# Layer 1's first norm in two halves, and three filter products moved into its gaps

## The reference

```
hl = modulate(rmsnorm(xl, norm1_g[l]), mod_l[0], mod_l[1])      # latent
hc = modulate(rmsnorm(xc, norm1_g[l]), mod_c[0], mod_c[1])      # context
hy_l, pool_l, cq_l, ckv_l, kpe_l = split(hl @ w_in[l])
hy_c, pool_c, cq_c, ckv_c, kpe_c = split(hc @ w_in[l])
k, v from ckv, kpe of both; attention, Hyena convolution and pooling, then w_out, gated residual add
rmsnorm, modulate, channel mixing: dense SwiGLU in layer 0, top-2 of 8 experts in layer 1
```

## Time and profile before

| | |
|---|---|
| median of 3 runs | 1709.87 us (1708.15 to 1710.27) |
| profiled execution | 1708.7 us, span 1706.8 us |
| TensorE matmul busy | 1618.1 us, 95% of the span |
| VectorE busy | 1294.3 us, 76% |
| ScalarE busy | 891.7 us, 52% |
| mean granted clock of TensorE | 0.977 of full speed |

### The profile page before, as it was taken

The page is one execution under the profiler, slowest core; times in us unless marked ns, Lnnn a source line. Parts: engine busy times, 40 slices in busy tenths (PEclk is TensorE's granted clock), DMA queues, the critical chain, the costliest instruction groups (busy, mean ns, idle before and its releaser), DMA issues.

```text
span 1706.8 us, 19495 instructions
## 1 busy us (share of the span) xinstructions
PE 1618.1 (95%) x7452; PEld 1273.2 (75%) x7452; DVE 1294.3 (76%) x1733; ACT 891.7 (52%) x1019; POOL 14.1 (1%) x30
## 2 busy tenths in 40 slices
PE   5998999899999999798789999999999999999996
PEld 2885668678788887685487778787887878788774
DVE  3844573797787756854668998898988889898897
ACT  3322372322222222434557777777777776777764
POOL 1000000000000000000000000000000000000000
PEclk9999999899999999899889999999999999999999
DMA  9226421444445553132137999999999999999992
GB/s 391 81 78 236 147 80 50 172 182 169 173 172 200 220 199 122 34 114 94 61 149 285 352 343 337 346 356 359 351 334 362 347 355 346 343 347 370 344 347 107
DMA packets 55971, 403.43 MB, mean 236 GB/s; under 512 B 6416, under 2 KB 6448, under 8 KB 8768
## 3 DMA queue, kind: packets, MB, share of 16 engines
q1 hardware_dynamic: 53712, 387.47, 60.5%
q0 software_dynamic: 2160, 14.63, 2.3%
HBM read 401.03 MB, written 1.05 MB: 236 GB/s over the span
## 4 chain that ended last, share of the span: by engine, by line
PE 76%; DVE 15%; ACT 5%; issue 3%; DMA 1%; SPq 0%; DVEq 0%; ACTq 0%
PE PS L439 20%; PE PS L441 20%; PE PS L440 20%; DVE w_lo L2254 6%; ACT w_hi L1480 3%; PE PS L737 2%; DVE arena L1616 1%; DVE w_lo L1603 1%; PE PS L993 1%; PE PS L762 1%; PE PS L749 1%; DMA arena<-in_ada 1%; PE PS L698 1%; PE PS L449 1%; PE PS L704 1%
## 5 line engine op out<-in xcount | busy, mean ns | idle before, releaser
L2254 DVE TENSOR_TENSOR w_lo<-arena,w_hi 128x2048 fp32r<-128x2048 f32 x132 | 301.7, 2290 | 43.9 <-ACT w_hi L1480 43.9
L2254 DVE TENSOR_TENSOR w_lo<-raw,w_hi 128x2048 fp32r<-128x2048 f32 x129 | 295.0, 2291 | 32.8 <-ACT w_hi L1480 32.4
L1480 ACT CAST w_hi<-arena 128x2048 fp32r<-128x2048 f32 x132 | 251.6, 1909 | 47.0 <-PE PS L441 47.0
L1480 ACT CAST w_hi<-raw 128x2048 fp32r<-128x2048 f32 x129 | 246.9, 1916 | 44.4 <-PE PS L441 44.4
L439 PE MATMUL PS<-hT_hi,w_hi 128*128 128x512 f32 (+1 forms) x576 | 217.6, 378 | 12.2 <-DVE hT_lo L1751 10.6
L440 PE MATMUL PS<-hT_lo,w_hi 128*128 128x512 f32 (+1 forms) x576 | 214.6, 373 | 0.0
L441 PE MATMUL PS<-hT_hi,w_lo 128*128 128x512 f32 (+1 forms) x576 | 214.4, 372 | 0.0
L439 PE MATMUL PS<-w_hi,hT_hi 128*128 128x512 f32 (+1 forms) x448 | 178.3, 398 | 0.3 <-DVE w_lo L2254 0.3
L441 PE MATMUL PS<-w_hi,hT_lo 128*128 128x512 f32 (+1 forms) x448 | 174.6, 390 | 0.0
L440 PE MATMUL PS<-w_lo,hT_hi 128*128 128x512 f32 (+1 forms) x448 | 173.5, 387 | 0.0
L1603 DVE TENSOR_TENSOR w_lo<-raw,w_hi 128x2048 fp32r<-128x2048 f32 (+1 forms) x54 | 122.3, 2266 | 34.8 <-ACT w_hi L1109 34.6
(11 more groups left out here) (320 smaller groups left out, 2520.2 us busy)
## 6 DMA issues: line engine op xcount, KB each, us to landing
raw<-in_moe SPq DMA_DIRECT2D x132, 1024.0 KB, 6.9
arena<-in_moe SPq DMA_DIRECT2D x132, 1024.0 KB, 6.9
raw<-in_ffn SPq DMA_DIRECT2D x33, 1024.0 KB, 4.8
raw<-in_dot SPq DMA_DIRECT2D x28, 1024.0 KB, 4.8
raw<-in_ada SPq DMA_DIRECT2D x17, 1024.0 KB, 7.3
raw<-in_out SPq DMA_DIRECT2D x8, 1024.0 KB, 4.8
raw<-in_inb SPq DMA_DIRECT2D x8, 960.0 KB, 4.8
raw<-in_ina SPq DMA_DIRECT2D x5, 1024.0 KB, 5.4
```

The costliest lines, as they stand in the source:

```text
L1480: nc.scalar.copy(w_hi[:, x_slot(j), :], x_raw(n)).then_inc(x_hi, 1)
L2254: v.tensor_tensor(w_lo[:, x_slot(j), :], x_raw(NGR * (i % 2) + j), w_hi[:, x_slot(j), :].bitcast(F32), ALU.subtract).then_inc(x_lo, 1)
```

## The change

- Layer 1's first norm treats the latent stream of all eight blocks, and the projection to u waits for these alone. The context's half is a second pass of the same code on ScalarE and VectorE, behind the convolutions and behind the split of the third B granule; ScalarE's shift copies come behind it.
- The B products with b = 1 take the latent tiles first, then the context's. Their PSUM banks are named outright; the spread's bank is now 7, since the context's pass still reads it. A context tile waits for the low halves of the four blocks that it reads.
- Steps 8 to 10 of layer 1's filter leave the feed-forward network: TensorE does step 8 ahead of the norm's column sums, step 9 between sums and spread, step 10 behind the spread. ScalarE's copies of step 8 stand behind the square root, those of 9 and 10 behind the latent half of the norm.
- Two calls that split weights within the norm go away, and events carry the stream's number.

```diff
-    return n if b % 3 == 0 and 3 <= n <= 10 else None
+    return n if b % 3 == 0 and 3 <= n <= 7 else None
...
+        def own_tiles(l, b):
+            return (0, 1, 2, 3) if l == 0 else (2, 3, 0, 1) if b else (2, 3)
...
-                b = 7 if l else None
+                b = {8: 0, 9: 3, 10: 2}.get(n, 7) if l else None
...
-                o = bank(f"rs {l} {w}", 7 if w == 2 else 6 if l else None)
+                o = bank(f"rs {l} {w}", 7 if w == 2 or l else None)
...
-                    eng.wait_ge(dve_done, after(f"hT {l} 1 {k}"))
+                    eng.wait_ge(dve_done, after(f"hT {l} 1 {k} 1"))
+                    if l == 0:
+                        eng.wait_ge(dve_done, after(f"hT 0 1 {k} 0"))
...
-                    ts = tiles_of(streams) if b == 0 else range(NT)
-                    os = {t: bank(f"B {l} {b} {t}") for t in ts}
+                    ts = own_tiles(l, b)
+                    os = {t: bank(f"B {l} {b} {t}", (6, 0, 1, 2, 3, 4)[2 * b + ts.index(t)] if l else None) for t in ts}
+                    if l:
+                        state["next"] = 5
...
+                            if l and t < 2:
+                                eng.wait_ge(dve_done, after(f"hT 1 1 {4 * half + 3} 0"))
...                                                        # TensorE, layer 1
                 if l:
+                    filters(1, 8)
                     norm_sum(l, 1, (0, 1))
+                    filters(1, 9)
                     norm_spread(l, 1, (0, 1))
+                    filters(1, 10)
                     state["next"] = 0
...                                                        # ScalarE, norm
-                    if k == 3 and (l, w) == (1, 1):
-                        upto(gindex[("ina", 1, 1, 0)])
...                                                        # ScalarE, project_in
                 else:
-                    eng.wait_ge(dve_done, after(f"t 1 1 {KD - 1} 0"))
+                    upto(gindex[("inb", 1, 2, 0)])
+                    norm(1, 1, (0,))
                     for k in range(KD):
                         act(shift_wide(k), ones[:, :], ACT.Copy, scale=mod[:, 1, 24 + k, 1:2])
...
-                    for t in (tiles_of(streams) if b == 0 else range(NT)):
+                    for t in own_tiles(l, b):
...                                                        # ScalarE, layer 1
-                norm(l, 1, (0, 1))
+                if l:
+                    filters(1, 8)
+                norm(l, 1, streams)
+                if l:
+                    filters(1, 9)
+                    filters(1, 10)
                 project_in(l, streams)
...                                                        # VectorE, norm
-                    if k == 4 and (l, w) == (1, 1):
-                        upto(gindex[("ina", 1, 1, 0)])
...                                                        # VectorE, project_in
                 upto(gindex[("inb", l, 2, 0)])
+                if l:
+                    norm(1, 1, (0,))
...
-                norm(l, 1, (0, 1))
+                norm(l, 1, streams)
```

More of the change, by code:

```diff
@@ L824, in gate_up @@
                         if f == 0:
-                            eng.wait_ge(dve_done, after(f"hT 0 2 {k}"))
+                            eng.wait_ge(dve_done, after(f"hT 0 2 {k} 1"))
                         for j, x in enumerate(fs):
@@ L1203, in norm @@
                         act(hT_hi[:, k, q], tb[:, k, q], ACT.Identity, bias=shift).then_inc(act_done, 1)
-                        did(f"hThi {l} {w} {k}")
-                    if k == 3 and (l, w) == (1, 1):
-                        upto(gindex[("ina", 1, 1, 0)])
+                        did(f"hThi {l} {w} {k} {s}")
             def project_in(l, streams):
@@ L1746, in norm @@
                     if k >= 0:
-                        eng.wait_ge(act_done, after(f"hThi {l} {w} {k}"))
+                        eng.wait_ge(act_done, after(f"hThi {l} {w} {k} {streams[-1]}"))
                         for s in streams:
@@ L1753, in norm @@
                                                    op0=ALU.add, op1=ALU.subtract).then_inc(dve_done, 1)
-                            did(f"hT {l} {w} {k}")
+                            did(f"hT {l} {w} {k} {s}")
             def project_in(l, streams):
```

## The result

| | before | after |
|---|---|---|
| median | 1709.01 us (4 runs) | 1699.91 us (1697.72 to 1701.08, 4 runs) |
| profiled execution | 1708.7, span 1706.8 | 1701.08, span 1699.2 |
| ratio of times, 95% interval | | 0.9949 [0.9936, 0.9961] |

The kernel is faster by 8.7 us by the ratio, where 5.5 were forecast from the rows. The interval of the first set, 6.7 to 10.9 us, leaves out the 5.5 that were forecast; that of the second, 4.4 to 9.2, holds it. So by the times alone the surplus is 1.3 to 3.2 us, and its causes have to be read from traces.

What follows compares the result with a forecast made beforehand. TensorE's matmul stream, 76% of the chain, was taken to bound the kernel. The terms -2.5 + 0.5 - 4.7 + 1.2 made -5.5 us; between two bases 1703.8 us was named, range 1701.0 to 1707.7.

Steps and rivals of the forecast that it cites:

- step 2: Filter products in the gaps of layer 1's first norm: 0.5 us lost, by the one between sums and spread.
- step 3: Norm ahead of layer 1's projection to u handles only the latent half, 0.79 us a block: 4.7 us gained.
- step 4: Context half behind the convolutions: ScalarE's queue delays the last weight granule's cast, stalling the B products: 1.2 us lost.
- Network: Feed-forward network: removing three filter products between gate/up groups and down projections gains 2.5 us, by group-start distances.
- warm case: Sums to norm: clock stays at full speed throughout, so the norm starts 1.1 us earlier.
- likeliest case: Sums to norm: clock falls once around the sums and returns, 0.2 to 0.8 us lost; 0.5 taken.
- cold bound: Sums to norm: sums, product and spread all at half clock, norm starts at 705.5, 2.4 us lost.
- warm rival: Norm's gaps at full clock throughout, gaining 1.1 us in place of losing 0.5: total -7.1, 1702.2 us; chance 0.20.
- The rival of a serial hand-over: Norm blocks run product, ScalarE, low half in series, at worst 1.46 us each: +3.9, 1713.2 us; chance 0.06.
- Tile order: B tiles in order 2, 3, 0, 1: VectorE's sums end 1.7 us later but stay covered: nothing, at most 1.7.
- shifts whole: Expert stage starts from layer 1's output and runs in a ring, so it moves with it; no size given.
- part 1: Three filter products leave the feed-forward network: 2.5 us gained, bounds 0.9 and 4.3.

Runs made afterwards that it cites:

- the second: Second set of seven executions of the changed kernel, unedited, against the kernel before: 0.9960 [0.9946, 0.9974], median 1700.49 us.
- bank alone: Kernel before, with layer 1's bank counter set to 5 in place of 4 behind the B products: 1704.67 us median, 0.9982.
- norm alone: Changed kernel with the three moved filter products put back in the feed-forward network: 1702.6 us median, 0.9956 against the kernel before.
- step 9 ahead: Changed kernel with the filter product between column sums and spread moved ahead of the sums: 1696.95 us median, 0.9930 against the kernel before.
- filters alone: Kernel before with only the three filter products moved into the norm's gaps: 1705.34 us median, 0.9981.
- shift copies behind: Changed kernel with ScalarE's eight shift copies behind the cast of the last B granule: 1700.13 us median, 0.9941 against the kernel before.
- bank free: Changed kernel with kpT in bank 4 and the last two cqT in banks 1 and 2: 1697.23 us median, 0.9929 against the kernel before.
- all three: Changed kernel with filter product moved ahead of sums, shift copies behind the cast, and kpT in bank 4: 1696.26 us median, 0.9924 against before.
- both repeats: Second runs on one chip: changed kernel unedited, 1700.49 us median; changed kernel with product, shift-copy and kpT-bank edits together, 1696.02 us.

## Why the prediction was wrong

**The direction and the place were right, and so was the mechanism of each listed part; the sum ended too early.** Its own stretches, 1 to 5, came to -5.1 us against -5.5 (the -5.4 down to the y products has 0.3 in it from the start of the kernel, which the change doesn't touch). That they are so close is partly luck: step 2 was off by +1.7, step 3 by -0.9 and step 4 by -0.3. By its steps:

1. *Network: -2.5 forecast, -2.54 measured*, and -2.45 to -2.55 in eight further traces with the products moved. Reading the price as the distance of group starts, not as the products' length of 4.3, was right; the 0.34 us stall came up in every group, as said.
2. *Norm's gaps: +0.5 forecast, +2.2 in the first trace.* The mechanism was right; the size changes from one execution to the next. Six traces with the product between sums and spread took 3.9, 3.9, 3.9, 5.6, 7.1 and 7.2 us for a stretch of 5.0 before: the forecast's warm case, its likeliest case and its cold bound all occurred, and their mean is +0.3. The 5.0 is itself one draw: with nothing between sums and spread it was 4.50 and 4.49 in the traces of bank alone and norm alone, where the clock fell a little later. The cases were right, but the chance of the warm one, 0.20, was low against three of six, and one fall seen at 365 us was too little to go by. The row that the warm rival rests on, layer 0's second norm with its sums at full clock, had a second half that wasn't read: the spread right behind those sums took 2.04 us (L542 at 308.43), so the clock fell there too, only later. The Trainium skill's sentence, page "TensorE: Matmul & The Clock Gate", Part 1, that "activity releases the throttle" fits step 9 ahead (1.00 up to the bursts, in two of the three traces with that edit) and the norm alone (0.50 in the projection where no products stand in the gaps). The third of those traces, where the clock fell behind the spread in spite of the products, and the changed kernel's, where it was 0.50 over 6.00 us of busy time, show that products in the gaps don't hold it up each time. The same part says that the number of matmuls that run cold differs between runs of one kernel; the changed kernel's two traces, 7.19 and 3.89 us, agree.
3. *Half norm: -4.7 forecast, -5.6 measured.* A misreading. I took the matmul at 715.03 for the eighth burst's; it is the seventh's, and the eighth starts at 715.85, the row that I used for a burst's length. Everything else of the step is in the trace: the low half 1.06 us behind its product, then 0.79 a block. VectorE's timeline after:

```profile
702.43 0.87 DVE L1757 SCALAR_TENSOR_TENSOR arena<-XT,gsc,PS 128x256 f32<-128x256 f32 x2 [3.92 <-PE PS L546]
703.49 0.48 DVE L1766 SCALAR_TENSOR_TENSOR hT_lo<-arena,mod,hT_hi 128x256 fp32r<-128x256 f32 x1 [0.18 <-ACT hT_hi L1216]
...
704.29 0.48 DVE L1766 SCALAR_TENSOR_TENSOR hT_lo<-arena,mod,hT_hi 128x256 fp32r<-128x256 f32 x1
```

   The eighth burst starts 7.15 us behind the norm's start, 7.2 forecast. The rival of a serial hand-over fell with these rows.
4. *Context half: +1.2 forecast, +0.92 measured*, with the stall where it was put, on ScalarE's order. Moving the shift copies took it away.
5. *Tile order: nothing forecast, nothing measured*: 10.54 us to the y products in both.

**The step that failed** is the one sentence in which the sum closes: that the expert stage "starts from layer 1's output" and all behind the y products "shifts whole". I walked through the diff's `state["next"] = 5` as if it were needed for correctness only and gave the bank numbers no cost. It changes which product waits for kpT's copies: the second to fourth before, the third and fourth after; and the first one waits for one copy of cqT fewer, 1.04 us in place of 1.40. That is 1.7 us of its own, and in the profiled execution 3.4, since the clock fell in the stall of 1.91 us before (in filters alone it didn't, behind a stall as long). These are the stretches before (PEclk is the third number from the end):

```profile
782.00:785.00 3.00, 1.20 (x3) 0.68 (x4) 0.00 (x0) 2.98 (x5) 0.00 (x0) 1.00 0.06 22
785.00:789.00 4.00, 4.00 (x6) 1.54 (x5) 2.29 (x1) 2.89 (x5) 0.00 (x0) 0.57 0.03 8
```

and not in the changed kernel, where no stall is over 1.1 us:

```profile
772.00:786.00 14.00, 12.40 (x37) 5.77 (x36) 4.88 (x7) 13.78 (x24) 0.00 (x0) 1.00 0.46 174
```

With the bank and the misreading in it, the sum would have been -2.5 + 0.5 - 5.6 + 1.2 - 1.7 to -3.4, so -8.1 to -9.8, and the time 1699 to 1701. The range's fast end, 1701.0, was the warm case and 1.2 us for part 1; nothing in it stood for a misread row or for a stretch that wasn't listed. In the second set of executions the surplus is 1.3 us only; what the bank is worth on average is known no closer than by bank alone, 1.4 to 5.0 us.

**What stays open.** Three stretches with unchanged instructions differ between traces by 1 to 2.5 us: the start up to layer 0's network (-0.7 to +2.4), the scores (40.9 to 42.3) and the output projection with the router (46.3 to 48.9). Behind the y products the two differences of the table are the clock's: in the scores the kernel before had 0.50 from 820 to 826 us where the changed one had 0.69 from 811 to 817, and in the output projection the changed kernel had 0.72 from 850 to 856 us where the projection before ran at 1.00. In the latter the clock fell although TensorE was busy for all of these 6 us and of the 10 before. Whether the change's timing makes such falls likelier isn't settled: that stretch was over 48 us in four of eight traces with both halves of the change (the changed kernel, shift copies behind, bank free, all three) and under 46.7 in the other four, among them both repeats; in the four traces without both halves it was never over 46.6.

## What to carry to other kernels

When a change reorders allocations (a bank counter set outright, one more or one less tile in a rotation), follow each later name to its new bank and ask what reads there last; a rotation by one was about a third of this gain. Price a moved piece by the distance between landmarks with and without it, and count the bursts of a row by name before you take a difference. Fill a gap only up to its length: the product that didn't fit cost 0.6 us at full clock (3.89 against 3.27) and up to 3.9 where the clock fell, and both products in the longer gap ahead cost nothing (48.87 us from the group to the sums, as before). Filling it isn't shown to hold the clock up: in one of three traces it fell behind the spread all the same.

## What the runs showed of the hardware

The spread between executions of one kernel is nearly as large as this change, and goes with the clock. Over the 43 executions of the kernel before that ran beside the experiments, times ranged from 1704.88 to 1711.48 us; the twelve with a mean granted clock of 0.977 or more averaged 1706.6, the seventeen with 0.974 or less 1709.8. Behind the same 2.16 us of idle time in front of the column sums the clock fell in three traces and not in three others, and in one trace it fell behind 0.45 and 0.98 us. The stretch from sums to norm took 3.9, 5.6 or 7.2 us with the same instructions, by whether and when the clock fell, and one trace shows one of these.
